# Fetching an expert's rows from DRAM by index instead of gathering them with one-hot products

## The reference, cut to what matters

```python
def moe_swiglu(x, w_router, w_in, w_out):
    """Top-2 of 8 SwiGLU experts, softmax over the selected logits (Mixtral)."""
    B, S, D = x.shape
    xt = x.reshape(B * S, D)
    logits = (xt @ w_router).astype(jnp.float32)
    top_v, top_i = lax.top_k(logits, TOP_K)
    top_w = jax.nn.softmax(top_v, axis=-1)
    gates = jnp.sum(jax.nn.one_hot(top_i, N_EXPERTS, dtype=jnp.float32) * top_w[..., None], axis=1)
    y = jnp.zeros_like(xt)
    for e in range(N_EXPERTS):
        y = y + gates[:, e:e + 1].astype(xt.dtype) * swiglu(xt, w_in[e], w_out[e])
    return y.reshape(B, S, D)
```

## Time and profile before

| what | value |
| --- | --- |
| runs shown | 2008.36, 2009.15, 2011.49 us |
| median | 2009.15 us |
| profiled execution | 2010.54 us, its span from first to last instruction 2008.8 us |
| PE busy | 1927.2 us (96%), 9064 matmul records |
| DVE busy | 1444.7 us (72%) |
| ACT busy | 1208.1 us (60%) |
| POOL busy | 13.4 us (1%) |
| moved by DMA | 502.35 MB, mean 250 GB/s; in the expert stage about 355 |
| granted clock of TensorE | 0.968 of full in the mean |

### The profile page before, as it was taken

One profiled execution on the slowest core, in us unless ns is written; L12 is line 12 of the kernel. 1 busy time (PEld: TensorE's weight loads), 2 busy tenths in 40 slices (PEclk: granted clock), 3 DMA queues, 4 the chain that ended last, 5 costly groups with the idle time before them and its releaser, 6 DMA issues.

```text
span 2008.8 us, 26117 instructions
## 1 busy us (share of the span) xinstructions
PE 1927.2 (96%) x9064; PEld 1609.0 (80%) x9064; DVE 1444.7 (72%) x1666; ACT 1208.1 (60%) x1278; POOL 13.4 (1%) x37
## 2 busy tenths in 40 slices
PE   7999999999988999999999999999999988979998
PEld 7998888887867888888888888888888866657886
DVE  5565555456657889888898888988888854557643
ACT  5544444457745777777777777777777744335542
POOL 2000000000000000000000000000000000000000
PEclk9999999999998999999999999999999998669999
DMA  8555565544357999999999999999999734015551
GB/s 255 177 181 209 181 196 189 182 153 147 105 208 257 376 335 367 374 327 377 334 366 359 342 373 332 371 348 355 372 332 371 271 116 147 1 41 179 175 182 42
DMA packets 233364, 502.35 MB, mean 250 GB/s; under 512 B 14156, under 2 KB 54176, under 8 KB 233296
## 3 DMA queue, kind: packets, MB, share of 16 engines
q1 hardware_dynamic: 232304, 499.70, 70.6%
q0 software_dynamic: 688, 0.70, 0.2%
q10 hardware_dynamic: 304, 1.05, 0.1%
HBM read 500.35 MB, written 1.05 MB: 250 GB/s over the span
## 4 chain that ended last, share of the span: by engine, by line
PE 87%; DVE 6%; ACT 4%; issue 2%; DMA 0%; ACTq 0%; DVEq 0%
PE G L1209 22%; PE G L1211 22%; PE G L1210 22%; PE SM L1209 4%; PE SM L1211 4%; PE SM L1210 4%; PE T L1171 3%; PE T L1538 1%; DVE work_r L2110 1%; ACT e_high L593 1%; DVE e_low L598 1%; ACT dense_high L411 1%; PE G L1645 1%; PE SM L1348 1%; DVE dense_low L422 0%
## 5 line engine op out<-in xcount | busy, mean ns | idle before, releaser
L598 DVE TENSOR_TENSOR e_low<-e_arrived,e_high 128x2048 fp32r<-128x2048 f32 x338 | 755.7, 2287 | 83.5 <-ACT e_high L593 83.0
L593 ACT CAST e_high<-e_arrived 128x2048 fp32r<-128x2048 f32 x338 | 624.2, 1911 | 3.4 <-PE SM L1211 3.0
L422 DVE TENSOR_TENSOR dense_low<-dense_raw,dense_high 128x2048 fp32r<-128x2048 f32 (+1 forms) x125 | 265.0, 2152 | 151.2 <-ACT dense_high L404 151.0
L1209 PE MATMUL G<-e_high,work_r 128*128 128x512 f32 x896 | 354.8, 396 | 3.7 <-DVE routing L2128 3.7
L1211 PE MATMUL G<-e_high,work_r 128*128 128x512 f32 x896 | 350.1, 391 | 0.0
L1210 PE MATMUL G<-e_low,work_r 128*128 128x512 f32 x896 | 349.3, 390 | 0.0
L1209 PE MATMUL G<-dense_high,xT_hi_all 128*128 128x512 f32 (+1 forms) x800 | 310.6, 388 | 14.8 <-DVE dense_low L422 9.8
L1211 PE MATMUL G<-dense_high,xT_lo_all 128*128 128x512 f32 (+1 forms) x800 | 301.3, 377 | 0.0
L1210 PE MATMUL G<-dense_low,xT_hi_all 128*128 128x512 f32 (+1 forms) x800 | 300.9, 376 | 0.0
L404 ACT CAST dense_high<-dense_raw 128x2048 fp32r<-128x2048 f32 (+1 forms) x125 | 219.8, 1798 | 96.2 <-PE G L1211 96.0
L1209 PEld LDWEIGHTS G<-e_high,work_r 128*128 128x128 f32 x896 | 168.7, 188 | 39.2 <-issue 3.9
(11 more groups left out here) (312 smaller groups left out, 1975.0 us busy)
## 6 DMA issues: line engine op xcount, KB each, us to landing
e_arrived<-in_m_w_in_dram SPq DMA_DIRECT2D x448, 512.0 KB, 4.8
e_arrived<-in_m_w_out_dram SPq DMA_DIRECT2D x224, 512.0 KB, 4.6
dense_raw<-in_a_w_in_dram SPq DMA_DIRECT2D x32, 768.0 KB, 4.7
dense_raw<-in_f_w_in_dram SPq DMA_DIRECT2D x44, 512.0 KB, 4.6
dense_raw<-in_w_up_dram SPq DMA_DIRECT2D x16, 1024.0 KB, 5.2
dense_raw<-in_w_down_dram SPq DMA_DIRECT2D x16, 1024.0 KB, 4.9
dense_raw<-in_a_w_out_dram SPq DMA_DIRECT2D x12, 1024.0 KB, 5.0
dense_raw<-in_f_w_out_dram SPq DMA_DIRECT2D x11, 1024.0 KB, 5.0
```

What stands on the lines that cost most here:

```text
L422: ins = nc.vector.tensor_tensor(unit_place(n, dense_low)[:, 0:4 * w], unit_place(n, dense_raw)[:, 0:4 * w], high_place(n)[:, 0:4 * w].bitc ...
L593: nc.scalar.copy(e_hi_unit(n), e_raw(n, e_arrived)).then_inc(e_hi, 1)
L598: nc.vector.tensor_tensor(e_raw(n, e_low), e_raw(n, e_arrived), e_hi_unit(n).bitcast(F32), ALU.subtract).then_inc(e_lo, 1)
L1209: nc.tensor.matmul(bank, x_hi, w_hi, start=start, stop=False)
```

## The change

The normed tokens are stored to DRAM once, ahead of the expert loop. For the next expert, PE multiplies the pick by a column of token numbers, which gives the token number of each slot (two products behind the last matmul of up 2, into T1). DVE turns that column into integers at its step for up 3. POOL then issues an indirect DMA that fetches the 128 rows into `xn`, and PE transposes them behind up 6, where the gather stood. The first expert still uses `gather`, and the next pick is still made, since the scatter needs it. The turn of chunk 2 into T1 now waits until the index has been copied.

```diff
--- before.py
+++ after.py
@@ -224,6 +224,9 @@
         indices = sb("indices", [P, 2, 8], U32)
         rounds_i = sb("rounds_i", [P, 2], I32)
         pos_i = sb("pos_i", [P, NT], I32)
+        token = sb("token", [P, NT])
+        token_of = sb("token_of", [P, 1], U32)
+        saved_rows = nc.dram_tensor("saved_rows", (S, D), F32, kind="Internal").ap()
         turn_i = sb("turn_i", [P, NT * ROPE_HALF], I32)
         rope = sb("rope", [P, 8, NT * ROPE_HALF])
 
@@ -484,6 +487,12 @@
         scatter_full = sem("scatter_full")
         scatter_added = sem("scatter_added")
         pick_ready = sem("pick_ready")
+        token_ready = sem("token_ready")
+        rows_saved = sem("rows_saved")
+        rows_asked = sem("rows_asked")
+        rows_landed = sem("rows_landed")
+        index_full = sem("index_full")
+        index_ready = sem("index_ready")
         e_turned = sem("e_turned")
         e_turned_hi = sem("e_turned_hi")
         e_turned_lo = sem("e_turned_lo")
@@ -770,6 +779,22 @@
             pool.dma_start(b_if[:, ML_H:2 * ML_H], t["b_fgate_2"].to_broadcast([P, ML_H])).then_inc(small_landed, 16)
             pool.dma_start(pos_i[:, :], t["positions_2"][0].rearrange("(c p) -> p c", p=P),
                           allow_slow_non_contiguous=True).then_inc(small_landed, 16)
+
+            nc.gpsimd.iota(token[:, :], pattern=[[P, NT]], base=0, channel_multiplier=1,
+                           allow_small_or_imprecise_dtypes=True).then_inc(token_ready, 1)
+            pool.wait_ge(xn_ready, NT)
+            for c in range(NT):
+                pool.dma_start(saved_rows[c * P:(c + 1) * P, :], xn[:, c, :]).then_inc(rows_saved, 16)
+            pool.wait_ge(rows_saved, 16 * NT)
+            pool.wait_ge(rounds_ready, 1)
+            rounds = pool.value_load(rounds_i[0:1, 0:1], min_val=1, max_val=2)
+            with pool.Fori(0, rounds * E) as it:
+                pool.wait_ge(index_ready, it + 1)
+                pool.wait_ge(gather_full, it * 2 + 2)
+                pool.sem_inc(rows_asked, 1)
+                pool.indirect_dma_start(xn[:, 0, :], None, saved_rows, bass.IndirectOffsetOnAxis(token_of[:, :], 0)
+                                        ).then_inc(rows_landed, 16)
+
 
 
         @block.scalar
@@ -1513,6 +1538,22 @@
                     if k % 4 == 3:
                         ins.then_inc(gather_full, 1)
 
+            def next_tokens(it):
+
+                pe.wait_ge(pick_ready, it + 2)
+                pe.wait_ge(e_turned_hi, it * len(TURNS) + TURN_OF["route"] + 1)
+                for c in range(NT):
+                    ins = nc.tensor.matmul(T[1][:, 0:1], pick[:, c, :], token[:, c:c + 1], start=(c == 0), stop=(c == NT - 1))
+                ins.then_inc(index_full, 1)
+
+            def turn_rows(it):
+
+                pe.wait_ge(rows_landed, it * 16 + 16)
+                for k in range(KD):
+                    ins = nc.tensor.transpose(G[2 + k // 4][:, k % 4 * P:(k % 4 + 1) * P], xn[:, 0, k * P:(k + 1) * P], ident[:, :])
+                    if k % 4 == 3:
+                        ins.then_inc(gather_full, 1)
+
             def scatter(c, full, banks):
 
                 for b in range(2):
@@ -1528,6 +1569,8 @@
                     pe.wait_ge(pick_ready, it + 1)
                     blocks = [pick[:, c, :] for c in range(NT)]
                 else:
+                    if what == 2:
+                        pe.wait_ge(index_ready, it + 1)
                     pe.wait_ge(up_read, it * UPS + what + 3)
                     blocks = [e_hid[:, what % 2, k * P:(k + 1) * P] for k in range(4)]
                 if g == 3:
@@ -1538,6 +1581,7 @@
                     ins = nc.tensor.transpose(T[g % 2][:, n * P:(n + 1) * P], src, ident[:, :])
                 ins.then_inc(e_turned, 1)
 
+            pe.wait_ge(token_ready, 1)
             pe.wait_ge(pick_ready, 1)
             pe.wait_ge(xn_ready, NT)
             gather(0)
@@ -1569,10 +1613,11 @@
                             e_turn(it, s - 1)
                             if s == 1:
                                 e_turn(it, "route")
+                        if s == 2 and part == 3:
+                            next_tokens(it)
                         if s == UPS - 1 and part == 3:
-                            pe.wait_ge(pick_ready, it + 2)
                             pe.wait_ge(up_read, it * UPS + (UPS - 2) + 3)
-                            gather(it + 1)
+                            turn_rows(it)
                     else:
                         if s == 0 and part == 0:
                             pe.wait_ge(scatter_added, it * 4 + 4)
@@ -2129,6 +2174,9 @@
             with dve.Fori(0, rounds * E) as it:
                 for n in range(0, UNITS, 2):
                     kind, s, part = UNITS_OF[n]
+                    if (kind, s, part) == ("up", 3, 0):
+                        dve.wait_ge(index_full, it + 1)
+                        V.tensor_copy(token_of[:, :], T[1][:, 0:1]).then_inc(index_ready, 1)
                     for ahead in (n + LEAD, n + LEAD + 1):
                         e_make_lo(dve, it, ahead)
                     if kind == "up" and s == 0:
```

## The result

The changed kernel takes 2068.51 us (median of 5 runs, 2066.68 to 2069.34), the kernel before 2010.7 beside it. The ratio is 1.0288 (95% interval 1.0274 to 1.0302): 58 us slower. Slower was forecast, but with 2054 us and a range up to 2065.

The account below looks back on a forecast made before the run. PE was taken to bound the kernel, DMA engines close behind. 2010.54 us profiled + 26.6 for the wait + 18 for the clock + 0 for the gather and the rest: 2055, so 2054 as median; range 2033 to 2065.

Parts of the forecast that it names:

- What bounds the stage: Expert stage: PE bounds, busy 123.7 of 124.0 us an expert, with the DMA engines close behind.
- The ceiling of 123.4 us an expert by the DMA engines: Expert stage: 44.5 MB at 361 GB/s take 123.4 us, so no expert can fall much below that.
- The gather against eight transposes: PE behind up 6: gather 3.60 us, eight transposes 0.88, so 2.72 us less PE work an expert.
- Where the 2.72 us go: Ahead of down 6: PE idles 3.03 us for DVE's low half of chunk 6; saving taken as 0.
- The new wait: PE behind up 2 waits for DVE's pick: 3.33 us an expert with the products, 26.6 in eight (22 to 30).
- The rest: Index copy on DVE, turn of chunk 2, ACT, SP, and POOL's stores and fetch: taken as 0.
- The clock: Expert stage: half clock behind twelve of sixteen gaps at 1.5 us each, 18 us; bounds 0 and 27.
- Rival 2: Both gaps in each expert: the clock falls every time at full price, 2063 us; chance 0.13.
- Rival 1: Behind up 2: the wait alone costs and the clock holds, 2036 us; chance 0.24 with few falls (2032 to 2046).
- Rival 3: ACT and DVE keep a lead while PE waits: faster, 0.6 us saved an expert, 2004 us; chance 0.03.
- Rival 4: Tail ahead of down 6: no stall, saving kept, 2014 to 2026 us with some clock falls; chance 0.03.
- The rows: Behind up 6: PE waits if the indirect load lands over 60 us late; at 65 us, 2094 us; chance 0.02.

Follow-up runs that it names:

- the best version: Changed kernel with index products behind down 1, ACT's chunk 6 copy before the gather copies, DVE's chunk 6 low half before down 6's second low half: 1989.94 us.
- the index products alone: Kernel before plus, behind up 2, the wait for the next pick and two unused one-column products; gather kept, nothing fetched: 2045.25 us.
- the filled version: Changed kernel plus matmuls of no use in both gaps, 11 during the wait for the pick and 13 ahead of down 6: 2036.34 us.
- the wait alone: Kernel before plus one PE wait for the next expert's pick behind up 2; nothing fetched, gather kept: 2038.39 us.
- the copies reordered: Changed kernel with ACT and DVE copying hidden chunk 6 ahead of the gather's copies; index products stay behind up 2: 2037.56 us.

## Why the prediction was right or wrong, point by point

- **What bounds the stage: right**, PE. The ceiling of 123.4 us an expert by the DMA engines was wrong: 361 GB/s was what one stretch had moved, not what they can; the best version moves 368, and SP still waits for PE there.
- **The gather against eight transposes: right in size.** 2.72 us was the estimate, 4.28 - 1.56 = 2.72 is what the trace of the changed kernel shows, and the best version returns it.
- **Where the 2.72 us go: right.** A gap of 3.03 us was forecast ahead of down 6, 3.00 is there, and down 6 starts when it did. Moving the low half to another place in the order of ACT and DVE gave the time back, so the cause is shown and not only read.
- **The new wait: right.** 3.33 us an expert forecast; 3.3 in the versions with filled gaps and with the index products alone (127.3 - 124.0), and 26 us of the result.
- **The rest at nothing: right.** The index copy takes 0.15 us on DVE, the rows land in 7.9 us, and the filled version, with the fetch, has the same expert of 127.3 us as the index products alone, without it.
- **The clock: the step that failed.** "Of sixteen gaps I let twelve be followed by it: 18 us. Bounds 0 and 16 x 1.7 = 27." All sixteen were, at 1.6 us each and not 1.5, which is 26; and four stretches were double, which no bound allowed for, another 6. Together 32 instead of 18. The upper end of the range was built on one stretch of 3.4 us a gap, and so lay too low. The mechanism was right, its term was mis-sized, and these 14 us are the miss: over the kernel before, 58 us were measured and 45 forecast. The trace of the kernel before had both warnings, which the prediction's comparison of three gaps left out: a stretch of 6.8 us behind a gap of 3.90, and, 3.0 us of matmuls behind the gap of 2.44 after which the clock had stayed, a gap of only 2.19 that half clock did follow:

```profile
1617.20:1623.90 6.70, 5.19 (x12) 4.02 (x13) 3.48 (x10) 1.16 (x5) 0.00 (x0) 0.50 0.01 4
...
1818.78 1.97 PE L1171 MATMUL T<-ident,h_all 128*128 128x128 f32 x8 [2.19 <-DVE h_all L2330]
...
1818.60:1821.90 3.30, 3.12 (x12) 2.83 (x13) 0.92 (x5) 1.96 (x8) 0.00 (x0) 0.50 0.00 0
```

- **The rivals.** Rival 2 (all gaps fall) was the right one, short of the double stretches. Rival 1 is what the filled version runs at: 2036.34 us against the 2036 worked out for it. Rival 3 (ACT and DVE keep a lead) did not come: both gaps have the same length in every expert. Rival 4 did not come either. The rows were not late.

The Trainium skill tells ("TensorE: Matmul & The Clock Gate", "HAM oscillation — how this bites in real kernels") of a kernel in which waits of some 3 to 5 us for a DMA brought half clock back in every tile. Here shorter gaps did it: 16 of 16 in the changed kernel, at 2.6 and 3.0 us, 4 of 8 at 2.6 us with the wait alone, and none of 8 at 0.93 us with the copies reordered.

Open is why gaps of 2.6 us were all followed by half clock in the changed kernel and only half of them with the wait alone. The index products by themselves gave 5 of 8. The second gap at full length is not needed: with the copies reordered it is 0.93 us, and all eight behind up 2 were still followed. What differs else is the distance between the gaps, and that was not varied by itself. In the changed kernel half clock began anywhere from 2.3 to 4.1 us after the start of its gap (at 1266.18 behind a gap that began at 1263.89, at 1320.80 behind one that began at 1316.70), so equal gaps differ in when the clock falls behind them.

## What to carry to other kernels

When work is taken from the bounding engine, look for what its next step waits for: if another engine's list runs without a hole from before the saved work to that step, the saving turns into idle time until that list is reordered. A small operation that consumes a result just made belongs as late in the engine's order as its own consumer allows; here down 1, 24 matmuls of 0.227 us, lay ready behind it. And an idle gap of 2 us or more between dense matmuls on TensorE (2.1 us: 13 of 16 here) should be priced with the half-clock stretch behind it (1.6 us here, 3 and more when double), which cost more in sum than the waits did.

## What the runs showed that was not expected

- Four of sixteen stretches of half clock lasted 6.8 us although PE worked without a pause once the gap was over (924.86 to 931.67, 18 matmul records). Three lie behind up 2, one ahead of down 6. In all four the clock fell while the gap or the index products behind it still lasted; of the twelve single ones, three fell so early too and nine later. What parts them in this trace is the time from the start of the gap to the fall: 2.30 to 2.67 us for the four, 2.73 to 4.10 for the twelve. With the wait alone, one stretch that began after 2.53 us stayed single, so it is no rule; it was not tested.
- Products that nobody reads made the kernel 32 us faster, by keeping the clock.
- Gaps of one length in one kernel do not all end alike: 4 of 8 at 2.6 us, 13 of 16 at 2.1 us, 4 of 16 at 1.6 us.
- The DMA engines went on to 368 GB/s with a share of 1.01, where before they showed a share of 1.00 at 361: a share of 1.00 did not mean that nothing was left.
